# Moving the experts' split weights, tokens and hidden values within SBUF

## The reference

```python
def expert_choice_ffn(h, router_w, w1, w3, w2):
    cap = EC_FACTOR * L // N_EXPERTS                       # 256 tokens for each of 16 experts
    aff = softmax(einsum('bld,de->ble', h, router_w))
    gate, idx = lax.top_k(swapaxes(aff, 1, 2), cap)
    xs = h[bidx, idx]
    hid = silu(einsum('becd,edf->becf', xs, w1)) * einsum('becd,edf->becf', xs, w3)
    y = einsum('becf,efd->becd', hid, w2) * gate[..., None]
    return zeros_like(h).at[bidx, idx].add(y)
```

## The kernel before, in words

| tile | first byte | behind a multiple of 256 |
|---|---|---|
| shi0 to shi3, then slo0 to slo3, 4096 bytes each | 121,600 and 137,984 | 0 |
| xs0, xs1 (gathered tokens) | 154,368 | 0 |
| xt_hi, xt_lo (tokens, 8192 bytes each) | 162,592 and 170,784 | 32 |
| ht_hi, ht_lo (hidden values, 8192 bytes each) | 179,200 and 187,392 | 0 |
| raw weights | 23,296 | 0 |

## Time and profile before

### The profile page before, as it was taken

The page is one execution under the profiler, slowest core; times in us unless marked ns, Lnnn a source line. Parts: engine busy times, 40 slices in busy tenths (PEclk is TensorE's granted clock), DMA queues, the critical chain, the costliest instruction groups (busy, mean ns, idle before and its releaser), DMA issues.

```text
span 2153.4 us, 35090 instructions
## 1 busy us (share of the span) xinstructions
PE 2074.0 (96%) x13569; PEld 1813.9 (84%) x13569; DVE 1370.2 (64%) x2082; ACT 996.3 (46%) x1630; POOL 278.0 (13%) x357
## 2 busy tenths in 40 slices
PE   6999999999999899997999999999999999999996
PEld 4778888888878677785999999999999999999985
DVE  3564548995994577757555656556555665656557
ACT  5923454444531445431444544445444444444455
POOL 0001100100001010020011112111221112111120
PEclk9999999999999999998999999999999999999998
DMA  7464333333327665456356666576565765657565
GB/s 258 150 240 136 112 107 99 114 113 94 125 76 237 235 209 178 144 213 257 118 207 243 218 217 208 190 259 214 196 218 191 273 203 186 216 214 258 196 230 225
DMA packets 188285, 407.95 MB, mean 189 GB/s; under 512 B 15956, under 2 KB 53396, under 8 KB 187300
## 3 DMA queue, kind: packets, MB, share of 16 engines
q1 hardware_dynamic: 162212, 318.36, 42.6%
q0 software_dynamic: 25984, 88.39, 12.6%
HBM read 329.59 MB, written 77.12 MB: 189 GB/s over the span
## 4 chain that ended last, share of the span: by engine, by line
PE 81%; DVE 10%; issue 3%; DMA 3%; ACT 2%; SPq 1%; POOL 0%; DVEq 0%; ACTq 0%; POOLq 0%
PE bh L55 11%; PE bh L57 11%; PE bh L56 11%; PE bank L55 8%; PE bank L57 8%; PE bank L56 8%; PE eby L55 5%; PE eby L57 5%; PE eby L56 5%; DVE acc L854 3%; PE ebt L2286 1%; PE bank L1037 1%; PE bank L1419 1%; DVE over L2018 1%; DVE raw L2474 1%
## 5 line engine op out<-in xcount | busy, mean ns | idle before, releaser
L55 PE MATMUL bh<-xt_hi,shi 128*128 128x256 f32 x2048 | 572.0, 279 | 3.0 <-DVE slo L2438 2.4
L56 PE MATMUL bh<-xt_lo,shi 128*128 128x256 f32 x2048 | 571.7, 279 | 0.0
L57 PE MATMUL bh<-xt_hi,slo 128*128 128x256 f32 x2048 | 571.7, 279 | 0.0
L2438 DVE TENSOR_TENSOR slo<-raw,shi 128x1024 fp32r<-128x1024 f32 x384 | 455.9, 1221 | 157.1 <-ACT shi L2348 153.0
L2348 ACT ACTIVATE shi<-raw 128x1024 fp32r<-128x1024 f32 x384 | 389.9, 1053 | 129.0 <-PE eby L57 127.2
L55 PEld LDWEIGHTS bh<-xt_hi,shi 128*128 128x128 f32 x2048 | 385.7, 188 | 4.2 <-issue 2.0
L56 PEld LDWEIGHTS bh<-xt_lo,shi 128*128 128x128 f32 x2048 | 385.8, 188 | 0.6
L57 PEld LDWEIGHTS bh<-xt_hi,slo 128*128 128x128 f32 x2048 | 385.8, 188 | 0.0
L55 PE MATMUL bank<-h_hi,whi 128*128 128x512 f32 x704 | 283.3, 402 | 0.0
L57 PE MATMUL bank<-h_hi,wlo 128*128 128x512 f32 x704 | 275.9, 392 | 0.0
L56 PE MATMUL bank<-h_lo,whi 128*128 128x512 f32 x704 | 275.7, 392 | 0.0
(11 more groups left out here) (347 smaller groups left out, 3121.7 us busy)
## 6 DMA issues: line engine op xcount, KB each, us to landing
raw<-in_exp_w_dram SPq DMA_DIRECT2D x96, 2048.0 KB, 11.1
uT<-stage POOLq DMA_DIRECT2D x72, 256.0 KB, 2.8
xb<-in_ada_w_dram SPq DMA_DIRECT2D x24, 512.0 KB, 6.0
wraw<-in_w_in_dram SPq DMA_DIRECT2D x22, 512.0 KB, 5.0
adaw<-in_ada_w_dram SPq DMA_DIRECT2D x8, 1024.0 KB, 10.1
xb<-in_x_dram SPq DMA_DIRECT2D x16, 512.0 KB, 4.4
xt<-in_x_dram POOLq DMA_DIRECT2D x16, 512.0 KB, 5.4
x2d<-xt POOLq DMA_DIRECT2D x16, 512.0 KB, 3.1
```

The source lines that it names most:

```text
L55: nc.tensor.matmul(out, w_hi, x_hi, start=start, stop=False)
L56: nc.tensor.matmul(out, w_hi, x_lo, start=False, stop=False)
L57: return nc.tensor.matmul(out, w_lo, x_hi, start=False, stop=stop)
L2438: nc.vector.tensor_tensor(item_dst(slo, n), item_src(n), item_dst(shi, n), ALU.subtract).then_inc(S["w_lo_ready"], 1)
```

## The change

The high and low tile of a slot now lie side by side, and the slots begin 32 bytes further on; the program names become functions of the item. The tiles of item 0 alone are placed 32 bytes lower than those of the other items that use slot 0. Two gaps are computed by `behind`, and four small tiles of the final norm become slices of one. ScalarE waits once for list_ready ahead of its split of item 3 of expert 0.

| tile | first byte | behind a multiple of 256 |
|---|---|---|
| slots 0 to 3: shi at, slo 4096 bytes on | 121,632 + 8192 for each slot | 32 |
| the same for item 0 of each expert | 121,600 | 0 |
| xs0, xs1 | 154,400 | 32 |
| xt_hi, xt_lo | 162,912 and 171,104 | 96 |
| ht_hi, ht_lo | 179,488 and 187,680 | 32 |

```diff
--- before.py
+++ after.py
@@ -1839,6 +1839,7 @@
         ada_loaded = [sem(f"r_ada{i}") for i in range(4)]
         v.aff_stored = S["aff_stored"]
         v.hot_free = (S["blocks_ready"], 1)
+        v.found_free = (S["list_ready"], 1)
 
         def by_half(ap):
             return ap.rearrange("p t (g e) -> p (t g) e", e=GE)
@@ -2129,13 +2130,36 @@
             return tile
 
         raw, raw_loaded = v.raw, v.s_raw
-        shi = [sb(f"shi{i}", [P, D], F32R) for i in range(NR)]
-        slo = [sb(f"slo{i}", [P, D], F32R) for i in range(NR)]
+
+        def behind(shift, unit):
+            at[0] += (shift - at[0]) % unit
+
+        at[0] += 32
+        halves = {}
+
+        def half_tile(name, offset):
+            return nc.alloc_sbuf_tensor_at(name, [P, D], F32R, offset=offset)
+
+        SHIFTED = {0: -32}
+        for slot in (0, 1, 2, 3):
+            halves[slot] = [half_tile(f"s{n}{slot}", at[0] + m * D * 4) for m, n in enumerate(("hi", "lo"))]
+            for item, shift in SHIFTED.items():
+                if item % NR == slot:
+                    halves[NR + item] = [half_tile(f"s{n}_of{item}", at[0] + shift + m * D * 4)
+                                         for m, n in enumerate(("hi", "lo"))]
+            at[0] += 2 * D * 4 + {}.get(slot, 0)
+
+        def shi(n):
+            return halves[NR + n if n in SHIFTED else n % NR][0]
+
+        def slo(n):
+            return halves[NR + n if n in SHIFTED else n % NR][1]
+
         xs_words = [sb(f"xs{i}", [P, D], F32R) for i in range(2)]
         xs = [t[:, :].bitcast(F32) for t in xs_words]
-        at[0] += 32
+        behind(96, 1024)
         xt_hi, xt_lo = sb("xt_hi", [P, KD, CAP], F32R), sb("xt_lo", [P, KD, CAP], F32R)
-        at[0] += 224
+        behind(32, 256)
         ht_hi, ht_lo = sb("ht_hi", [P, FD, CAP], F32R), sb("ht_lo", [P, FD, CAP], F32R)
         sil = [sb(f"sil{i}", [P, CAP]) for i in range(2)]
         hft = [sb(f"hft{i}", [P, CAP]) for i in range(2)]
@@ -2143,7 +2167,8 @@
         pause = sb("epause", [P, 2])
         gates = [sb(f"gates{i}", [P, NE]) for i in range(2)]
         fw, junk = sb("fw", [P, D]), sb("fjunk", [P, D])
-        ssq, msq, rst, nt = (sb("f_" + n, [P, NT + 2]) for n in ("ssq", "msq", "rst", "nt"))
+        small = sb("f_small", [P, 4 * (NT + 2)])
+        ssq, msq, rst, nt = (small[:, i * (NT + 2):(i + 1) * (NT + 2)] for i in range(4))
         spare = [sb(f"spare{i}", [P, D]) for i in range(3)]
         gidx = v.gidx
         sidx = [sb(f"sidx{i}", [P, 1], U32) for i in range(2)]
@@ -2173,7 +2198,7 @@
             return t[:, :, (n // 2 % 4) * P:(n // 2 % 4 + 1) * P] if n < 16 else t[:, (n - 16) % 4, :]
 
         def item_dst(buf, n):
-            ap = buf[n % NR][:, :]
+            ap = buf(n)[:, :]
             return ap.rearrange("p (k c) -> p k c", k=KD) if n < 16 else ap
 
         def group(t):
@@ -2290,7 +2315,7 @@
                 def down(f, s, half):
                     c, w, n = slice(s * P, (s + 1) * P), slice(half * 512, (half + 1) * 512), 16 + f
                     return mm3(nc, by[2 * s + half][:, :], ht_hi[:, f, c], ht_lo[:, f, c],
-                               shi[n % NR][:, w], slo[n % NR][:, w], start=(f == 0), stop=(f == FD - 1))
+                               shi(n)[:, w], slo(n)[:, w], start=(f == 0), stop=(f == FD - 1))
 
                 def body(e, first, last_e):
                     pe.wait_ge(S["x_lo_ready"], e * 4 + 4)
@@ -2301,7 +2326,7 @@
                             pe.wait_ge(S["w_lo_ready"], e * NI + (n + 1))
                             for k in range(KD):
                                 c = slice(k * P, (k + 1) * P)
-                                last = mm3(nc, bh[f % 2][:, m * CAP:(m + 1) * CAP], shi[n % NR][:, c], slo[n % NR][:, c],
+                                last = mm3(nc, bh[f % 2][:, m * CAP:(m + 1) * CAP], shi(n)[:, c], slo(n)[:, c],
                                            xt_hi[:, k, :], xt_lo[:, k, :], start=(k == 0), stop=(k == KD - 1))
                             last.then_inc(S["item_multiplied"], 1)
                     if not last_e:
@@ -2418,6 +2443,8 @@
 
                 act.wait_ge(*v.hot_free)
                 for n in range(NR):
+                    if n == NR - 1:
+                        act.wait_ge(*v.found_free)
                     split(0, n)
                 for j in range(4):
                     tok_hi(0, j)
```

## The result

The changed kernel takes 2163.15 us (median of 10 runs, 2160.19 to 2165.40), the kernel before 2155.47 us (10 runs, 2152.47 to 2159.14): a ratio of 1.0037, 95% interval 1.0027 to 1.0046. It is slower, by 7.7 us, where the forecast was 2136 us.

What follows compares the result with a forecast made beforehand. The prediction took the distances between TensorE's matmul starts as the bound. Its terms, -18.0 - 2.4 + 0 - 0.5 = -20.9 us, gave 2134.2 us for the profiled execution and a forecast median of 2136 us, range 2121 to 2177.

Steps and rivals of the forecast that it cites:

- The bound: Experts, 1040 to 2060 us: the time is the sum of distances between TensorE's matmul starts, and nothing else.
- Items 1 to 15: Up stage, tokens 64 bytes further behind than weights: 113.33 ns a matmul instead of 116.67, -18.0 us (bounds -54 and +18).
- rows 5 and 6: Profile rows: up stage, tokens 32 bytes behind, 116.67 ns a matmul; context projection, both operands at a multiple, 120.00 ns.
- Item 0: Up stage, weights at 0 and tokens at 96: 110.00 ns a matmul, -2.4 us (bounds -3.6 and +1.2).
- The down stage: Both operands go from 0 to 32, distance stays 0: 226.67 ns unchanged, 0 us (bounds -4.8 and +4.8).
- The splits: ScalarE and VectorE writing weights and tokens to moved destinations: a start at 32 shows no penalty, cost 0.
- the wait: ScalarE's added wait for list_ready: over 1.5 us before it is asked for, cost 0.
- the last expert: Only 16.41 us, 142 matmuls, of it profit, since its chain goes through a load of rows: -0.5 us.
- Rival 1: Up stage: distance repeats after 64 bytes, items 1 to 15 at 120.00 ns, +18.4 us, 2175 us; chance 0.27.
- Rival 2: Moving operand's place counts, not distance: 2152 us with down stage alone (0.13), about 2113 with up stage too (0.12).
- Rival 3: All stages: addresses do not matter, 2157 us, within the scatter; chance 0.13.

Runs made afterwards that it cites:

- first map: Changed kernel with split weights at 0, 32, 64, 96 by item number modulo 4, tokens at 96, hidden values at 0: 2164.8 us (one run).
- second map: Changed kernel with split weights at 0, 32, 64, 96 by item number modulo 4, but tokens at 32: 2168.2 us (one run).
- kernel with four items moved: Changed kernel with items 0, 4, 8, 12 at 0, 96, 64, 0 and slots from 1 on 256 bytes further: 2146.7 us (one run).

## Why the prediction was wrong

**The bound** was read rightly: the time of the experts is the sum of the distances between matmul starts. 7.10 us more there are the 7.0 us of the span, and no wait took their place.

**Items 1 to 15** are the step that failed, as a mechanism and not only in size: "I take one more step like the one that rows 5 and 6 show ... 113.33 ns". Measured were 117.78 ns, 5400 x 1.11 = +6.0 us where the sum had -18.0. It lies within the bounds that the text gave (106.67 to 120.00), but the step was a line through two points. The level of 113.33 exists for this distance; two levels do, and the change's items get the upper one. That one pair of places could have two lasting levels was in none of the cases.

**Item 0** failed the same way: 110.00 ns forecast, 120.0 measured, 360 x 3.33 = +1.2 us where the sum had -2.4, at its upper bound.

**The down stage** was right: distance 0 before and after, 226.67 ns. The map shows that this was no indifference.

**The splits, the wait and the last expert** were right: 1222 and 1054 ns, no idle time of ScalarE for list_ready, and a tail that moves with TensorE (75.65 us behind the load of rows, 76.06 before). The kernel with high beside low alone bears out the first two at a ratio of 1.0000.

**Rival 1**, slower by a return to 120.0 ns after 64 bytes, had the sign; its mechanism is not what runs showed, since items 1 to 15 stand at 117.78 and item 0, for which it gave 116.67, at 120.0. **Rival 2** falls with the second map: both at 32 reads as both at 0. **Rival 3**, addresses don't matter, falls with the maps. The prediction had made this rival out of a rule of the Trainium skill ("TensorE: Matmul & The Clock Gate", Part 2, step-by-step), that a weight load takes nothing from a running matmul. The traces speak against what the prediction drew from it, that addresses don't matter: 32 bytes of a tile's place change the pace by up to 6.67 ns a matmul. The same page of the Trainium skill ("Back-to-back issue gap") gives columns / 2.4 + 2.5 ns, by estimate 109.2 ns for 256 columns. No state here reached it.

**Chances.** 0.28 stood on slower. The time lies inside the range, but that is luck and no merit of the sum: the range reached so far up only for rival 1, whose mechanism the runs refute.

What stays open: why distance 0 leads to the lower state of distance 64 and distance 32 does not, which hold-ups change the state, what the down stage and the turns hand to item 0, and which accesses meet in SBUF. On the last but one: from the second expert on, item 1 (behind item 0 at distance 96) reads 113.33 ns in the first map, whose down stage has mixed places, and 117.78 in the kernel with four items moved, whose down stage is at distance 0 throughout. No run measures the weight loads alone. Distances other than -64 to 96 were not tried, nor was a lower state searched for in the down stage or in the projections.

## What to carry to other kernels

Where TensorE is the bound and every matmul comes with its own weight load, measure starts over 24 or more matmuls for each placement of the two operands, and don't extrapolate a placement effect beyond the distances measured: here 0, 32, 64 and 96 bytes read 120.0, 116.67, 113.33 or 117.78, and 120.0 ns. Measure each placement in its real neighbourhood too: what an earlier stretch leaves behind can last for hundreds of matmuls, and one deliberately slow item of 24 matmuls at the head of each expert paid for itself many times. That holds while TensorE isn't held up; a wait can undo it.

## What the runs showed of the hardware that was not expected

One instruction stream has two lasting paces: 256 columns moving, 128 stationary, float32r, tokens 64 bytes further behind a multiple of 256 than the weights, 113.33 or 117.78 ns a matmul at the full granted clock. Where TensorE isn't held up, a state holds for 15 items, 360 matmuls, on end, and the lower one outlasts items at distances of 32 and 96; it came alike in the first 15 experts. 24 matmuls at distance 0 lead to the lower one, and a hold-up of TensorE changed it both ways. With the lower pace an expert takes 66.92 us instead of 68.06, for no matmul more or less. And the stage with 512 moving columns, 226.67 ns at distance 0, loses when its moving operand stands at four places by turns: 236.8 against 232.0 ns of busy time for each matmul in the map.

At the lower of TensorE's two clock levels, 1.2 GHz, the part that placement changes is gone. In the changed kernel the granted clock fell to 0.50 in the last expert, about 0.7 us after TensorE had taken up work again behind a wait of 1.87 us:

```profile
2105.30:2107.30 2.00, 2.00 (x12) 2.00 (x11) 1.52 (x4) 1.39 (x3) 0.00 (x0) 0.50 0.03 8
```

```profile
2105.34 0.41 PE L56 MATMUL bh<-xt_lo,shi 128*128 128x256 f32 x1
...
2107.26 0.41 PE L56 MATMUL bh<-xt_lo,shi 128*128 128x256 f32 x1
```

Nine matmuls take 1.92 us, 213.3 ns each: 256 cycles of 1.2 GHz for 256 columns and nothing on top, at distance 64. The kernel before, at distance 32, takes the same 213.3 ns (2098.35 to 2100.27 us, clock 0.50), where at the full clock the two differ by 1.11 ns.
